# A language-model layer step on one Trainium2 core: the last part of the down-projection and the last norm in four column blocks of 258 instead of three of 344

## The reference, cut to what matters

```python
def conv_ffn(x, w_up, conv_w, conv_b, w_down, buf):
    up = x @ w_up                                   # 2 x 2816 columns
    h = conv_b + sum(padded[:, j:j + T] * conv_w[j] for j in range(3))
    val, gate = jnp.split(h, 2, axis=-1)
    out = (jax.nn.silu(gate) * val) @ w_down        # 2816 -> 1024
    return out, padded[:, -2:]
...
ff, nb = conv_ffn(x, ...)
x = layer_norm(ALPHA * x + ff, ln2_g[l], ln2_b[l])  # mean, variance over the 1024 features, then g, b
```

## Time and profile before

| | |
|---|---|
| median of 3 runs | 1242.88 us |
| the profiled execution's own time | 1241.75 us |
| its span in the trace | 1240.0 us |
| PE busy | 1207.9 us (97% of the span) |
| VectorE, ScalarE, GpSimd busy | 833.5, 502.6, 170.5 us |
| chain that ended last, whole span | PE 87%, VectorE 9%, ScalarE 1% |
| the part touched by the change | from 1151 us to the end, 89 us |

### The profile page before, as it was taken

How to read it: one execution, slowest core, us unless ns; L and a number is a source line. 1 busy time by engine, 2 the same in 40 slices (tenths; PEclk the granted TensorE clock), 3 DMA queues, 4 the chain that set the end, 5 groups by cost and what they waited for, 6 DMA issues and landing times.

```text
span 1240.0 us, 21885 instructions
## 1 busy us (share of the span) xinstructions
PE 1207.9 (97%) x8628; PEld 1162.7 (94%) x8628; DVE 833.5 (67%) x1520; ACT 502.6 (41%) x836; POOL 170.5 (14%) x143
## 2 busy tenths in 40 slices
PE   7999999999989999998999999999999999999996
PEld 7988888999889999998999999999999999999995
DVE  6896767575788648599744884488447853786545
ACT  5411111235466425666522552255215531454335
POOL 6210000000000034310020003000300030001352
PEclk9999999999899999999999999999999999999999
DMA  8331322526524521221264125512551255212512
GB/s 291 117 105 45 86 71 79 173 86 158 115 78 122 207 104 34 92 82 52 60 208 164 53 54 193 183 38 68 174 188 55 53 161 199 70 54 59 200 37 101
DMA packets 82902, 138.61 MB, mean 112 GB/s; under 512 B 24992, under 2 KB 50592, under 8 KB 82792
## 3 DMA queue, kind: packets, MB, share of 16 engines
q1 hardware_dynamic: 82800, 137.21, 34.7%
HBM read 96.67 MB, written 39.50 MB: 110 GB/s over the span
## 4 chain that ended last, share of the span: by engine, by line
PE 87%; DVE 9%; issue 2%; ACT 1%; DMA 1%; SPq 0%; ACTq 0%; DVEq 0%
PE psum L1856 31%; PE psum L1828 15%; PE psum L1571 15%; PE psum L1939 5%; PE psum L1590 5%; PE psum L1637 4%; PE psum L1717 2%; PE psum L1560 1%; PE psum L1688 1%; PE psum L1684 1%; DVE R L2451 1%; DVE SC L2271 1%; PE psum L1672 1%; DVE K L2256 1%; PE psum L1648 1%
## 5 line engine op out<-in xcount | busy, mean ns | idle before, releaser
L1856 PE MATMUL psum<-XH,wh 128*128 128x258 f32 x640 | 181.3, 283 | 1.7 <-ACT ub L1278 1.4
L1856 PE MATMUL psum<-XH,wl 128*128 128x258 f32 x640 | 181.0, 283 | 0.0
L1856 PE MATMUL psum<-TR,wh 128*128 128x258 f32 x640 | 180.9, 283 | 0.0
L1856 PE MATMUL psum<-XL,wh 128*128 128x258 f32 x640 | 179.9, 282 | 0.3 <-issue 0.3
L1522 POOL TENSOR_TENSOR wl<-raw,wh 128x512 fp32r<-128x512 f32 (+2 forms) x36 | 57.8, 1611 | 568.1 <-ACT wh L1227 557.4
L1856 PEld LDWEIGHTS psum<-XH,wh 128*128 128x128 f32 x640 | 121.0, 189 | 2.3 <-issue 2.3
L1828 PE MATMUL psum<-AH,wl 128*128 128x344 f32 x384 | 123.1, 320 | 0.0
L1828 PE MATMUL psum<-AL,wh 128*128 128x344 f32 x384 | 123.0, 320 | 0.0
L1828 PE MATMUL psum<-AH,wh 128*128 128x344 f32 x384 | 122.9, 320 | 0.0
L1856 PEld LDWEIGHTS psum<-XL,wh 128*128 128x128 f32 x640 | 121.5, 190 | 0.5 <-issue 0.5
L1856 PEld LDWEIGHTS psum<-XH,wl 128*128 128x128 f32 x640 | 120.9, 189 | 0.0
(11 more groups left out here) (379 smaller groups left out, 2897.9 us busy)
## 6 DMA issues: line engine op xcount, KB each, us to landing
raw<-in_w_up SPq DMA_DIRECT2D x44, 512.0 KB, 4.2
ub<-rscr SPq DMA_DIRECT2D x16, 516.0 KB, 5.1
rscr<-ub SPq DMA_DIRECT2D x16, 516.0 KB, 3.9
raw<-in_w_dn SPq DMA_DIRECT2D x32, 256.0 KB, 3.3
raw<-in_w_units SPq DMA_DIRECT2D x15, 512.0 KB, 4.4
fscr<-st SPq DMA_DIRECT2D x10, 516.0 KB, 2.9
R<-in_xT SPq DMA_DIRECT2D x8, 516.0 KB, 6.9
RS<-rscr SPq DMA_DIRECT2D x8, 516.0 KB, 4.4
```

The lines of the kernel that those rows point to most:

```text
L1856: ins = nc.tensor.matmul(psum[:, bank, 0:QW], a[:, k * P:(k + 1) * P], x, start=(start and p_ == 0), stop=(stop and p_ == 2), skip_group_c ...
```

## The change

The last part of the down-projection and the last norm work in `LB = 4` blocks of `QW = 258` columns. Six groups are still held, but they are now (0,0) to (0,3), (1,0) and (1,1); the others follow block by block, so row tile 1 also comes up in blocks 2 and 3. That makes 32 groups. The hand-written places move with it; the new ones are the same pattern once more for the added block.

```diff
-LAST = [(m, b) for m in range(2) for b in range(NB)] + [(m, b) for b in range(NB) for m in range(2, KD)]
-HELD = 2 * NB
+LB = 4
+HELD = 6
+LAST = [(i // LB, i % LB) for i in range(HELD)] + [(m, b) for b in range(LB) for m in range(1, KD) if LB * m + b >= HELD]
-LAST_BANKS = [3 * m + b for m, b in LAST[:HELD]]
+LAST_BANKS = list(range(HELD))
+        def last_square(n):
+            if n >= KD * (LB - 1) + SQ_SLOTS:
+                return hb[1][:, quarter(n % KD - SQ_SLOTS)]
+            return ub[n % SQ_SLOTS // NB][:, blk(n % NB)][:, 0:QW]
...
 SP
-            for b in range(NB):
+            for b in range(LB):
                 for m in range(KD):
                     sp.wait_ge(y_ready, KD * b + m + 1)
-                    sp.dma_start(yT[m][:, blk(b)], R[:, m, blk(b)]).then_inc(y_out, 16)
+                    sp.dma_start(yT[m][:, quarter(b)], R[:, m, quarter(b)]).then_inc(y_out, 16)
...
 ScalarE (squares, inverse, affine: blk -> quarter, 0:CW -> 0:QW)
-            act.wait_ge(mean2, NB - 1)
             squares(2)
             inverse(2)
             affine(2)
+            act.wait_ge(mean2, LB - 1)
+            squares(3)
+            inverse(3)
+            affine(3)
...
 GpSimd (sums of rows and of squares: blk -> quarter)
-                    if b and m == 3 - b:
+                    if b and m == max(1, 3 - b):
                         for k in range(1, 5):
                             add_squares(b - 1, k)
...
 PE
-                        last = nc.tensor.matmul(psum[:, bank, 0:CW], w, gated(x, k)[:, blk(b)],
+                        last = nc.tensor.matmul(psum[:, bank, 0:QW], w, gated(x, k)[:, quarter(b)],
...
-                if i == NB:
+                if i == 3:
                     pe.wait_ge(mix, mix_count(JT - 1, "C211"))
...
-                if (m, b) in ((2, 2), (5, 2)):
+                if b > 1 and m in (1, 5):
                     group(i, range(2))
-                    (mean if m == 2 else variance)(1)
+                    (mean if m == 1 else variance)(b - 1)
                     group(i, range(2, nk))
...
-            mean(NB - 1)
-            pe.wait_ge(rstd2, NB - 1)
+            mean(LB - 1)
+            pe.wait_ge(rstd2, LB - 1)
             for m in range(KD):
-                last = nc.tensor.matmul(psum[:, 7, 0:CW], ones_ln[:, :], square(KD * (NB - 1) + m), start=(m == 0), stop=(m == KD - 1))
+                last = nc.tensor.matmul(psum[:, 7, 0:QW], ones_ln[:, :], last_square(KD * (LB - 1) + m), start=(m == 0), stop=(m == KD - 1))
...
 VectorE (evacuation, center, add_last_squares, scale: blk -> quarter, 0:CW -> 0:QW)
-                elif (m, b) == (3, 2):
-                    add_last_squares(1)
-                elif (m, b) == (4, 2):
-                    scale(1)
-            center(NB - 1)
-            scale(NB - 1)
+                elif b > 1 and m == 3:
+                    add_last_squares(b - 1)
+                elif b > 1 and m == 4:
+                    scale(b - 1)
+                elif (m, b) == (7, 2):
+                    center(2)
+            center(LB - 1)
+            scale(LB - 1)
```

More of the change, by code:

```diff
@@ L1415, in squares @@
                     n = KD * b + m - SQ_SLOTS
-                    if 0 <= n < KD * (NB - 1) and n % KD < 5:
+                    if 0 <= n < KD * (LB - 1) and n % KD < 5:
                         act.wait_ge(sq_used, 4 * (n // KD) + max(n % KD, 1))
-                    elif 0 <= n < KD * (NB - 1):
+                    elif 0 <= n < KD * (LB - 1):
                         act.wait_ge(sq_high, 2 * (NB + n // KD) + max(n % KD - 5, 1))
-                    me(act.activation(square(KD * b + m), R[:, m, blk(b)], ACT.Square), sq2)
+                    me(act.activation(last_square(KD * b + m), R[:, m, quarter(b)], ACT.Square), sq2)
             def inverse(b):
                 act.wait_ge(var2, b + 1)
-                me(act.activation(hb[0][:, blk(b)], psum[:, 7, 0:CW], ACT.Ln, bias=eps_ln[:, :]))
+                me(act.activation(hb[0][:, quarter(b)], psum[:, 7, 0:QW], ACT.Ln, bias=eps_ln[:, :]))
                 me.sync()
-                me(act.activation(hb[0][:, blk(b)], hb[0][:, blk(b)], ACT.Exp, scale=-0.5), rstd2)
+                me(act.activation(hb[0][:, quarter(b)], hb[0][:, quarter(b)], ACT.Exp, scale=-0.5), rstd2)
             def affine(b):
@@ L1430, in affine @@
                     act.wait_ge(t2, KD * b + m + 1)
-                    me(act.activation(R[:, m, blk(b)], R[:, m, blk(b)], ACT.Identity,
+                    me(act.activation(R[:, m, quarter(b)], R[:, m, quarter(b)], ACT.Identity,
                                       scale=ln_sb[:, 2, m:m + 1], bias=ln_sb[:, 3, m:m + 1]), y_ready)
@@ L1534, in add_squares @@
                 pool.wait_ge(sq2, KD * b + m + 1)
-                a = sqacc[:, 0, :]
+                a = sqacc[:, 0, 0:QW]
                 if m == 1 and b:
                     pool.wait_ge(var2, b)
-                pool.tensor_tensor(a, square(KD * b) if m == 1 else a, square(KD * b + m), ALU.add).then_inc(sq_used, 1)
+                pool.tensor_tensor(a, last_square(KD * b) if m == 1 else a, last_square(KD * b + m), ALU.add).then_inc(sq_used, 1)
                 pool.wait_ge(sq_used, 4 * b + m)
-            for b in range(NB):
-                acc = hb[1][:, blk(b)]
+            for b in range(LB):
+                acc = hb[1][:, quarter(b)]
                 for m in range(1, KD - 1):
@@ L1947, in mean @@
                     pe.wait_ge(xc2, KD * b)
-                nc.tensor.matmul(psum[:, 6, 0:CW], ones_ln[:, :], hb[1][:, blk(b)], start=True, stop=False)
+                nc.tensor.matmul(psum[:, 6, 0:QW], ones_ln[:, :], hb[1][:, quarter(b)], start=True, stop=False)
                 pe.wait_ge(*evacuated_last(KD - 1, b))
-                nc.tensor.matmul(psum[:, 6, 0:CW], ones_ln[:, :], R[:, KD - 1, blk(b)], start=False, stop=True).then_inc(mean2, 1)
+                nc.tensor.matmul(psum[:, 6, 0:QW], ones_ln[:, :], R[:, KD - 1, quarter(b)], start=False, stop=True).then_inc(mean2, 1)
             def variance(b):
@@ L1955, in variance @@
                     pe.wait_ge(rstd2, b)
-                nc.tensor.matmul(psum[:, 7, 0:CW], ones_ln[:, :], sqacc[:, 0, :], start=True, stop=False)
+                nc.tensor.matmul(psum[:, 7, 0:QW], ones_ln[:, :], sqacc[:, 0, 0:QW], start=True, stop=False)
                 pe.wait_ge(sq_high, 2 * (NB + b + 1))
-                nc.tensor.matmul(psum[:, 7, 0:CW], ones_ln[:, :], sqacc[:, 1, :], start=False, stop=True).then_inc(var2, 1)
+                nc.tensor.matmul(psum[:, 7, 0:QW], ones_ln[:, :], sqacc[:, 1, 0:QW], start=False, stop=True).then_inc(var2, 1)
             for i in range(HELD):
@@ L2640, in center @@
                     dve.wait_ge(*evacuated_last(m, b))
-                    me(TT(R[:, m, blk(b)], R[:, m, blk(b)], psum[:, 6, 0:CW], ALU.subtract), xc2)
+                    me(TT(R[:, m, quarter(b)], R[:, m, quarter(b)], psum[:, 6, 0:QW], ALU.subtract), xc2)
             def add_last_squares(b):
-                a = sqacc[:, 1, :]
+                a = sqacc[:, 1, 0:QW]
                 if b:
@@ L2650, in add_last_squares @@
                         dve.wait_ge(sq_high, 2 * (NB + b) + 1)
-                    TT(a, square(KD * b + 5) if m == 6 else a, square(KD * b + m), ALU.add).then_inc(sq_high, 1)
+                    TT(a, last_square(KD * b + 5) if m == 6 else a, last_square(KD * b + m), ALU.add).then_inc(sq_high, 1)
             def scale(b, ms=range(KD)):
@@ L2656, in scale @@
                     dve.wait_ge(xc2, KD * b + m + 1)
-                    me(TT(R[:, m, blk(b)], R[:, m, blk(b)], hb[0][:, blk(b)], ALU.mult), t2)
+                    me(TT(R[:, m, quarter(b)], R[:, m, quarter(b)], hb[0][:, quarter(b)], ALU.mult), t2)
             for i, (m, b) in enumerate(LAST):
@@ L2661, in _ @@
                 dve.wait_ge(row_in[m], 64)
-                me(TT(R[:, m, blk(b)], R[:, m, blk(b)], psum[:, LAST_BANKS[i % HELD], 0:CW], ALU.add), last_evac)
+                me(TT(R[:, m, quarter(b)], R[:, m, quarter(b)], psum[:, LAST_BANKS[i % HELD], 0:QW], ALU.add), last_evac)
                 if (m, b) == (3, 1):
```

6 lines of the change are left out of this document (3 added, 3 removed).

## The result

The changed kernel takes 1246.53 us (median of 8 runs, 1245.08 to 1247.2), the kernel before 1242.3 in the same comparison. The ratio is 1.0034, with a 95% interval of 1.0025 to 1.0043: slower by 0.34%, 4.2 us. The forecast was 1246.8 us, which is +3.95 us on the median of 1242.88 known then. The profiled execution took 1247.2 us, its span 1245.1.

The account below looks back on a forecast made before the run. Bound: PE's gapless stream to 1223.87 us, then a 16.1 us serial tail. Stream +6.35 (1.1 + 0.6 + 2.9 + 1.7), last mean +0.1, tail -2.5: +3.95 us on the 1242.88 median, 1246.8 us; range 1244.2 to 1249.4.

Parts of the forecast that it names:

- Steps 1 and 2: Last part on PE: 576 narrower matmuls instead of 432, +1.1 us; six mean or variance pairs instead of four, +0.6 us.
- step 1: Matmuls of the last part: 432 at 157.8 ns become 576 at 120.3 ns, +1.1 us, from some 14 ns fixed each.
- Step 3: Held groups, start of the last part: being narrower, they leave PE waiting 2.9 us for gated tile 21.
- Step 4: Block 0: PE waits 1.4 us for the weights of m = 6 and 0.3 us for m = 7.
- Step 5: Waits inside the last part's stream: all hidden except 0.1 us at the last mean, for GpSimd's two row sums.
- Step 6: Serial tail after the last group: all its work on 258 columns instead of 344, -2.5 us.
- (b): Tail shrinks by a full quarter, 4.0 us, with waits at their lower ends: +1.2 us, 1244.1; chance 0.12.
- (a): PE's waits for tile 21 and the later weights are covered and do not come: -0.8 us, 1242.1; chance 0.06.
- (c): PE's clock halves for 6.8 us after tile 21's wait: +1.7 us more, 1248.5, or 1250.2 if later; chance 0.15.

Follow-up runs that it names:

- held8: The changed kernel with eight groups held instead of six: 1242.58 us, ratio 1.0010 against the kernel before.
- after2: The changed kernel once more, without an edit: 1247.0 us, ratio 1.0043 against the kernel before.
- null: The kernel before once more, without an edit: 1243.06 us, ratio 1.0016 against the kernel before.
- null2: The kernel before again without an edit, in a later comparison: 1242.8 us, ratio 1.0006 against the kernel before.
- held4: The changed kernel with four groups held instead of six: 1249.72 us, ratio 1.0067 against the kernel before.
- order6: The changed kernel with group (2,1) moved ahead of (6,0) in block 0: 1244.63 us, ratio 1.0030 against the kernel before.
- narrow3c: The kernel before with three blocks of 388, 386 and 258 columns, variance(0) earlier and scale pieces spread out: 1241.66 us, ratio 1.0000.

## Why the prediction was right, step by step

The forecast of +3.95 us stands against +4.2 between the medians: +3.60 in the stage, +0.3 outside the span, and some 0.3 before the stage, where nothing was changed and where runs of one kernel differ by more than that (last section). The stage itself came out 0.35 us below the forecast.

- **Steps 1 and 2** (forecast +1.1 and +0.6). The distance is 119.9 to 120.0 ns, as the prediction took from the up-projection. A pair of fp32 matmuls by ones takes 0.43 to 0.45 us a piece, 0.87 a pair. held8, where nothing waits, measures the two steps and what small waits are left together: +1.98 (72.72 to 74.70). Its second-last mean took 0.66 instead of 0.43 us for the first matmul and its last mean started 0.1 late, so +1.7 is left, as forecast. The reason that step 1 gives for its +1.1 is loose: 144 more matmuls with 14 ns each that do not shrink would be +2.0. The two distances themselves give (157.8 - 120.3) / 86 = 0.436 ns a column and 120.3 - 258 x 0.436 = 7.8 ns that do not shrink, and 144 x 7.8 ns is the +1.1. The formula of the Trainium skill that the prediction set beside the trace ("TensorE: Matmul & The Clock Gate", Back-to-back issue gap) would have made the first step +0.4. It is given there for isolated matmuls, and the measured distance, with a weight load for each, does not agree with it: 120 ns for 258 columns, where an estimate by the page is 258 / 2.4 + 2.5 = 110.
- **Step 3** (2.9 us). Measured 2.8, by the producer that was named. The premise, that nothing in the change touches the tile's producers, held: from the last evacuation of the up-projection to the start of the tile's low part it is 12.24 us before (1151.15 to 1163.39) and 12.23 after (1152.65 to 1164.88).
- **Step 4** (1.4 + 0.3). Mis-sized: the listed wait for m = 6 is 0.8. Counted from start to start, as the prediction did, it is 1178.03 - (1166.17 + 90 x 0.120) = 1.06 against 1.4. The weights were ready 1177.97 - 1166.11 = 11.86 us after tile 21, before it was 1176.87 - 1164.62 = 12.25. The split for m = 6 hangs on a load, which landed 0.4 us sooner. The lower bound of the step (m = 6 ready 0.4 earlier) was what came. The wait for m = 7, with the restart, is the 9.12 - 8.63 = 0.5 us of the chain. Steps 3 and 4 together and the restarts are 4.0 us (78.70 - 74.70), against 2.9 + 1.7 = 4.6.
- **Step 5** (0.1 us). GpSimd's last sums end at 1231.29, the last mean starts at 1231.35, V + 5.87 with V = 1225.48; PE could ask at V + 5.77. A wait of 0.1 us. The view of waits lists 0.3 for the weight load of this matmul, since that one asks earlier.
- **Step 6** (-2.5 us). Measured 16.13 to 13.75, -2.38. The matmuls by ones give 4.88 - 3.73 = 1.15 us (forecast 1.2), the affine steps 8 x (0.583 - 0.514) = 0.55 (0.57). The groups by line and form of the changed kernel bear out the slopes drawn from the earlier trace rows:

```profile
L2672 DVE TENSOR_TENSOR R<-R,psum 128x258 f32<-128x258 f32 x32 | 13.0, 422 | 24.5 <-PE psum L1949 24.3
...
L1427 ACT ACTIVATE ub<-R 128x258 f32<-128x258 f32 x30 | 10.2, 413 | 16.9 <-DVE R L2651 11.2 <-POOL RS L1548 3.7 <-PE psum L1960 2.0
```

422 ns instead of the 424 taken, and 413 against 483 - 71 = 412. A quarter off the columns is 18% off VectorE's instruction (512 to 422) and 14% off ScalarE's (483 to 413), which is why rival (b), the whole tail by a quarter, did not come.

**What was not foreseen.** The time outside the span grew by 0.3 us, and the prediction had no term for it. It stands against a stage that came out 0.35 us below the forecast, most of it in step 4. The two errors cancel, so the total is closer than the terms are, and that part of the agreement is luck.

**The rivals.** (a) fell: both waits came. It was one step away, though. With two more groups held its case came too: held8's stage is -0.46, where (a) had -0.8. (b) fell. (c) is half right: absent in one profile of the changed kernel, present in the next. There it added 0.24 us to the stage, not 1.7: the stretch was half as long as the 6.8 us assumed, and the waits of step 4 took up most of the 1.5 us that it cost. Two of the seven runs of after2 took 1250.5 us at a mean granted clock of 0.990 and 0.991; whether their fall lay here or earlier cannot be told, as they have no trace.

## What to carry to other kernels

Cutting blocks to shorten a serial tail also cuts the work that hides the last inputs: count the held work in microseconds, not in groups (k = 0 to 4 of six groups, the work ahead of the last tile, was 6 x 15 x 157.8 ns = 14.2 us of matmuls and became 10.8 at 120.3 ns), and set it against the arrival of the latest input and of each weight before the cut. Where the stream's bound is a fixed arrival, the work taken away less the margin before gives the new wait: here 3.4 - 0.55 = 2.8 us, as measured. If the number of banks allows it, hold more groups in the same edit: in the stage, with eight of them the narrower blocks cost nothing, with four they cost 8.5 us, 3.0 of them by the clock. Even with eight the change did not beat the kernel before.

## What the runs showed that was not expected

**The clock falls in one execution and not in the next.** Near 334 us, long before the change, the granted clock is at one half for a stretch that differs from profile to profile of the kernel before: 6.84 us in the first, 13.7 us in null, none in null2. Windows of null, then one of null2:

```profile
335.00:336.00 1.00, 1.00 (x11) 1.00 (x10) 0.00 (x0) 0.64 (x3) 0.00 (x0) 1.00 0.00 0
336.00:337.00 1.00, 1.00 (x8) 1.00 (x6) 0.00 (x0) 0.98 (x4) 0.00 (x0) 0.52 0.33 71
...
349.00:350.00 1.00, 1.00 (x5) 0.93 (x4) 0.93 (x3) 1.00 (x5) 0.00 (x0) 0.65 0.00 0
```
```profile
325.00:360.00 35.00, 30.26 (x236) 28.84 (x235) 28.92 (x50) 21.54 (x35) 0.00 (x0) 1.00 0.34 101
```

In null the clock falls while PE is busy in the whole window and in the one before it. The start of the stage lies at 1148.61 us in null2, 1151.15 in the first profile and 1157.07 in null. These stretches are not the whole of it: null is 2.2 us late already near 320 us (the same instruction of VectorE, line 2256, starts at 321.85 us instead of 319.69), with the clock at 1.00 up to there, and it has one more stretch of 3.4 us between 388 and 396. Over the runs of the kernel before beside null2, the time goes with the mean clock: 1239.5 us at 0.998, 1241.6 at 0.995, 1244.0 at 0.992. But one run of null, at a mean of 0.946, took 1241.67, so the mean clock does not always tell. A change of 0.1 to 0.3% is therefore better read from the stage than from the span.

**A wait of PE can cost more than its length.** After 6.4 us (held4, one profile) the clock was at one half for 10 us; after 2.8 us it was so in after2 and not in the first profile of the same kernel nor in order6; in narrow3c it fell in the serial tail while PE made its matmuls by ones, through which it stayed at 1.00 in all other profiles. No run here tells what decides it.

**The time outside the span** is 0.3 us longer in all kernels with four blocks, and the stores are not the reason.
